# Mixture-of-experts layer on one core: down weights of an expert in one 4 MB transfer, the first chunk of the input projection by products, and new orders of units

## The reference

```python
h = rmsnorm(x, g_mix)
proj = h @ w_in                              # (256,1024) @ (1024,2048): u | q | k | v
y_pool = causal_multiscale_pool(u, w_pool, pool_scale)
y_attn = dilated_attention(q, k, v)          # 8 heads, three (window, dilation) patterns
x = x + concat(y_pool, y_attn) @ w_out
h2 = rmsnorm(x, g_ffn)
# top-4 of 32 experts for each token, softmax over the chosen logits -> combine[token, expert]
for e in range(32):
    gu = h2 @ w_gu[e] + b_gu[e]              # (256,1024) @ (1024,2048)
    gate = minimum(gu[:, :1024], 7); lin = clip(gu[:, 1024:], -7, 7)
    act = gate * sigmoid(1.702 * gate) * (lin + 1)
    out = out + combine[:, e:e+1] * (act @ w_down[e] + b_down[e])
return rmsnorm(x + out, g_final)
```

## Time and profile before

| | |
|---|---|
| time, median of 3 executions | 1023.37 us (1023.37 to 1024.65) |
| the profiled execution: its time | 1022.32 us |
| its span, first to last instruction | 1020.5 us |
| mean granted TensorE clock, share of full speed | 0.979 |
| TensorE busy | 957.0 us, 94% |
| VectorE, ScalarE busy | 285.6 us, 134.8 us |
| moved by DMA | 419.53 MB, 411 GB/s over the span |

### The profile page before, as it was taken

How to read it: one execution, slowest core, us unless ns; L and a number is a source line. 1 busy time by engine, 2 the same in 40 slices (tenths; PEclk the granted TensorE clock), 3 DMA queues, 4 the chain that set the end, 5 groups by cost and what they waited for, 6 DMA issues and landing times.

```text
span 1020.5 us, 11711 instructions
## 1 busy us (share of the span) xinstructions
PE 957.0 (94%) x4837; PEld 421.8 (41%) x4837; DVE 285.6 (28%) x536; ACT 134.8 (13%) x200; POOL 15.1 (1%) x17
## 2 busy tenths in 40 slices
PE   8999999999999998989899899989999898999996
PEld 8988443434343342424243243424324243434332
DVE  5963521313122113113122212212211311222123
ACT  6634200000101000000000000000100000010002
POOL 0500000000000000000000000000000000000000
PEclk9999999999999999999999899989999999999999
DMA  9578999999999999999999999999999999999995
GB/s 354 218 325 363 396 407 416 426 423 431 435 427 430 432 430 429 430 431 433 432 429 432 432 425 432 432 437 432 432 429 432 424 430 432 437 424 430 425 426 206
DMA packets 26321, 419.53 MB, mean 411 GB/s; under 512 B 4164, under 2 KB 4824, under 8 KB 8856
## 3 DMA queue, kind: packets, MB, share of 16 engines
q1 hardware_dynamic: 26256, 419.15, 96.8%
q10 hardware_dynamic: 40, 0.01, 0.0%
HBM read 418.11 MB, written 1.05 MB: 411 GB/s over the span
## 4 chain that ended last, share of the span: by engine, by line
PE 51%; DMA 44%; DVE 3%; ACT 1%; issue 0%; SPq 0%; DVEq 0%; ACTq 0%
PE ps L988 49%; DMA raw<-in_w_gu 40%; DMA raw<-in_w_down 3%; DVE woutl L720 1%; PE ps L1284 1%; PE ps L1234 1%; DMA win<-in_w_in 1%; ACT sm L538 0%; PE ps L1081 0%; DVE mxs L737 0%; DVE sm L732 0%; DVE xT L816 0%; PE ps L1135 0%; DVE acc L967 0%; DVE outs L970 0%
## 5 line engine op out<-in xcount | busy, mean ns | idle before, releaser
L988 PE MATMUL ps<-raw,xT 128*64 128x512 f32 x2032 | 469.8, 614 | 34.1 <-DMA raw<-in_w_gu 34.1
L988 PEld LDWEIGHTS ps<-raw,xT 128*64 128x64 f32 x2032 | 144.3, 141 | 339.2 <-issue 292.8
L988 PE MATMUL ps<-raw,actT 128*64 128x512 f32 x1024 | 232.1, 595 | 0.7 <-DMA raw<-in_w_down 0.7
L988 PEld LDWEIGHTS ps<-raw,actT 128*64 128x64 f32 x1024 | 70.6, 137 | 135.0 <-issue 132.4
L911 DVE TENSOR_TENSOR biased<-ps,biasT 128x1024 f32<-128x1024 f32 x32 | 39.2, 1224 | 304.1 <-PE ps L1234 304.1
L604 ACT ACTIVATE gu<-ps 128x1024 f32<-128x1024 f32 x32 | 32.8, 1025 | 551.2 <-PE ps L988 551.2
L928 DVE TENSOR_TENSOR acc<-ps,acc 128x512 f32<-128x512 f32 x60 | 38.8, 686 | 168.8 <-PE ps L988 168.8
L816 DVE TENSOR_TENSOR xT<-ps,gT 128x512 f32<-128x512 f32 x32 | 22.1, 692 | 166.0 <-PE ps L988 165.9
L988 PE MATMUL ps<-ysc,dispT 64*128 64x512 f32 x256 | 65.5, 613 | 0.9 <-ACT ysc L616 0.9
L988 PEld LDWEIGHTS ps<-disp,h 128*128 128x128 f32 x512 | 58.4, 192 | 12.4 <-issue 12.2
L988 PE MATMUL ps<-disp,h 128*128 128x128 f32 x512 | 61.7, 278 | 0.2 <-DVE disp L810 0.2
(11 more groups left out here) (161 smaller groups left out, 440.3 us busy)
## 6 DMA issues: line engine op xcount, KB each, us to landing
raw<-in_w_gu SPq DMA_DIRECT2D x57, 4096.0 KB, 33.2
raw<-in_w_down SPq DMA_DIRECT2D x63, 2048.0 KB, 31.4
raw<-in_w_gu SPq DMA_DIRECT2D x13, 2048.0 KB, 12.8
win<-in_w_in SPq DMA_DIRECT2D x16, 512.0 KB, 12.4
wout<-in_w_out SPq DMA_DIRECT2D x4, 1024.0 KB, 10.0
early<-in_w_gu SPq DMA_DIRECT2D x1, 2048.0 KB, 12.2
raw<-in_w_down SPq DMA_DIRECT2D x2, 1024.0 KB, 36.8
acc<-in_x SPq DMA_DIRECT2D x2, 512.0 KB, 4.0
```

Source lines behind the costliest of these rows:

```text
L988: return pe.matmul(out_, lhsT, rhs, start=start, stop=stop, skip_group_check=shared)
```

## The change

Seven things change.

1. **Down weights whole.** Where the two down units of an expert lie in neighbouring buffers (`whole_down`), `load_down_whole` fetches both in one 4 MB transfer with rows of 32 KB. It waits until the second of the two buffers is free, and TensorE's `down_unit` waits for the whole before the first unit. This holds for four of the six down loads of three pairs, the last expert's excepted, and for the one of pair 0, half 1: 20 of the 32 experts in all.
2. **First chunk by products.** `first_chunk` does all high-by-high products of chunk 0 first, then those with `hTl`, then those with `winl`, and waits for each part only when its products come. ScalarE and VectorE take the split of weight chunk 1 before the second part of the input.
3. **Chunks 0 and 1 of pair 0's second expert** are multiplied before the transposes of the routing weights and of the first gate-and-up result.
4. **The first piece for pair 1** comes in two halves of 1 MB (`load_halves`): the first is issued once chunk 0 is used (`half_unit`), the second once the unit is.
5. **Pair 1's second expert** comes in four 2 MB pieces (`small_next=second_loaded`) where two transfers of 4 MB stood.
6. **Down unit (0, 1) ahead of the wait for `xT_ready`** and of `turn_gu`, in all pairs but the last. In the last pair, down (1, 0) goes ahead of the wait for `outputs_ready` and the first `last_scatter`.
7. **The first three pairs of the loop are written out**, and the loop runs from 1: three rounds where four were.

```diff
+        def whole_down(third, half):
+            return buffer(0, third, 10 if half else 4) < RAW - 1
...
+            def load_halves(e, s):
+                src = w_gu[0, bass.ds(e, 1), 0:4 * P, :].rearrange("a (p r) n -> p (a r) n", r=4)
+                sp.wait_ge(half_unit, 1)
+                sp.dma_start(raw[:, s, 0, :], src[:, 0, :]).then_inc(halves_loaded[0], 16)
+                sp.wait_ge(unit_used, 1)
+                sp.dma_start(raw[:, s, 1, :], src[:, 1, :]).then_inc(halves_loaded[1], 16)
...
+            def load_down_whole(e, s, half):
+                sp.dma_start(raw[:, s:s + 2].rearrange("p b r n -> p (b r n)"),
+                             w_down[0, bass.ds(e, 1), :, :].rearrange("a (p r) n -> p (a r n)", r=8)).then_inc(
+                                 down_whole[half], 16)
...
+                elif j is None or whole_down(third, 1):
+                    free(i, k + 1)
+                    load_down_whole(a + 1, at_(k), 1)
                 else:
                     for u in range(DN_U):
                         down(a + 1, u, k + u, down_loaded[1])
                 if not last:
                     gate_up(nxt + 1, ITER_U, 1, small_next)
-                    down(nxt, 0, ITER_U + GU_U, down_loaded[0])
-            iteration(None, 0, small=third_loaded)
+                    if j is None or whole_down((third + 1) % 3, 0):
+                        free(i, ITER_U + GU_U + 1)
+                        load_down_whole(nxt, at_(ITER_U + GU_U), 0)
+                    else:
+                        down(nxt, 0, ITER_U + GU_U, down_loaded[0])
+            iteration(None, 0, small=third_loaded, small_next=second_loaded)
...
-            with sp.Fori(0, triples) as j:
+            for third in range(3):
+                iteration(0, third)
+            with sp.Fori(1, triples) as j:
...
             turned_high(0)
             win_part(0, 0)
+            win_part(0, 1)
             turned_high(1)
-            win_part(0, 1)
+            win_part(0, 2)
             turned_high(2)
+            win_part(0, 3)
             turned_high(3)
-            for c in range(2, 5):
-                win_part(0, c)
+            win_part(0, 4)
...
+            def first_chunk(parts):
+                for product, (w, x_) in enumerate(((winh, hTh), (winh, hTl), (winl, hTh))):
+                    if product == 1:
+                        pe.wait_ge(hTl_ready, 1)
+                    if product == 2:
+                        pe.wait_ge(win_low[0], 1)
+                    for bank, column in parts:
+                        for j in range(4):
+                            mm(ps[:, bank + j // 2, (j % 2) * T:(j % 2 + 1) * T],
+                               w[0][0][:, column + j * P:column + (j + 1) * P], x_[:, 0, :],
+                               start=product == 0 and j % 2 == 0, stop=False, shared=True)
...
+                ins = gu_unit(0, c, None if c >= 6 else 1 + c // 2, 1)
+                if c == 0:
+                    ins.then_inc(half_unit, 1)
+            for c in range(2):
+                gu_unit(1, c, buffer(None, 0, 0), 1, second_loaded)
...
-                    if k == 1:
+                    if k == (2 if first else 1):
                         pe.wait_ge(gate_clipped, i * 2 + 1)
                         pe.wait_ge(up_clipped, i * 2 + 1)
...
                     gather(1)
+                    down_unit(0, 1, buffer(j, third, 5), j, third)
                     pe.wait_ge(xT_ready, i * 2 + 4)
+                    turn_gu(i * 2 + 1)
                 else:
                     pe.wait_ge(dispT_ready, i + 1)
                     pe.wait_ge(added, i * 4 - 4 + (TT + 4))
-                turn_gu(i * 2 + 1)
-                down_unit(0, 1, buffer(j, third, 5), i + 1)
+                    turn_gu(i * 2 + 1)
+                    down_unit(0, 1, buffer(j, third, 5), j, third)
...
                 if last:
+                    down_unit(1, 0, buffer(j, third, 10 - gap), j, third, last=True)
                     pe.wait_ge(outputs_ready, i * 2 + 1)
                     last_scatter(0, 0)
-                    down_unit(1, 0, buffer(j, third, 10 - gap), i + 1, last=True)
-                    down_unit(1, 1, buffer(j, third, 11 - gap), i + 1, last=True)
+                    down_unit(1, 1, buffer(j, third, 11 - gap), j, third, last=True)
                     last_scatter(0, 1)
```

More of the change, by code:

```diff
@@ L392, in gate_up @@
                     if loaded is not None:
-                        for k in range(GU_U):
+                        if j is None and half == 0:
+                            load_halves(e, at_(first))
+                        for k in range(j is None and half == 0, GU_U):
                             free(i, first + k)
@@ L405, in iteration @@
                 k = GU_U
-                if j is not None:
+                if j is not None and not whole_down(third, 0):
                     down(a, 1, k + 1, down_loaded[0])
@@ L1005, in by_channel @@
             def by_channel(c, bank, h, column):
-                first, last = c == 0, c == DC - 1
+                last = c == DC - 1
                 for j in range(4):
@@ L1026, in _ @@
             pe.wait_ge(vec_ready, 1)
-            for c in range(DC):
+            pe.wait_ge(hTh_ready, 1)
+            pe.wait_ge(win_high[0], 1)
+            first_chunk(((6, DP), (4, 0)))
+            for c in range(1, DC):
                 pe.wait_ge(hTl_ready, c // 2 + 1)
@@ L1200, in gu_unit @@
                 r = c % 2
-                if pieces is not None:
+                if pieces is third_loaded and c < 2:
+                    pe.wait_ge(halves_loaded[r], 16)
+                elif pieces is not None:
                     if r == 0:
-                        pe.wait_ge(pieces[c // 2], 16)
+                        pe.wait_ge(pieces[c // 2], count * 16)
                 elif c % 4 == 0:
@@ L1260, in _, with iteration @@
             triples = pe.snap(pe.value_load(further[0:1, 0:1], min_val=0, max_val=MORE) + 4)
-            def iteration(j, third, last, first=False, biases=False):
+            def iteration(j, third, last, first=False, biases=False, pieces=None):
                 i = number(j, third)
                 for k in range(DC):
-                    gu_unit(1, k, buffer(j, third, k // 2), i, second_loaded if first else last_loaded if last else None)
-                    if k == 1:
+                    if not (first and k < 2):
+                        gu_unit(1, k, buffer(j, third, k // 2), pieces or i - 1, second_loaded if pieces else None)
+                    if k == (2 if first else 1):
                         pe.wait_ge(gate_clipped, i * 2 + 1)
@@ L1328, in last_scatter @@
                         ins.then_inc(scattered, 1)
-            iteration(None, 0, False, first=True)
-            with pe.Fori(0, triples) as j:
+            iteration(None, 0, False, first=True, pieces=1)
+            iteration(0, 0, False, pieces=2)
+            iteration(0, 1, False)
+            iteration(0, 2, False)
+            with pe.Fori(1, triples) as j:
                 for third in range(3):
```

42 lines of the change are left out of this document (28 added, 14 removed).

## The result

| | before | after |
|---|---|---|
| median | 1022.5 us (20 runs beside the change) | 1024.61 us (1022.37 to 1026.55, 20 runs) |
| ratio | | 1.002, 95% interval 1.0013 to 1.0026 |
| profiled execution: time | 1022.32 us | 1025.99 us |
| its span | 1020.5 us | 1024.2 us |
| mean granted clock | 0.979 | 0.982 |

The account below looks back on a forecast made before the run. The weight stream was taken to set the pace, TensorE close behind. From the profiled 1022.32 us, -1.3 - 1.1 - 1.6 + 0.7 + 2.0 gave 1021.0, plus 1.05 for the median: 1022.1 us, range 1018.0 to 1025.2.

Parts of the forecast that it names:

- Term 1: At the start, TensorE's first product begins at about 10.6 us instead of 11.94, shifting the whole stream: -1.3 us.
- Term 2: Weight stream from 105 to 177 us: 4.4 us of losses before, a new 3.3 us hole after: -1.1 us.
- Term 3: Down weights in 32 KB rows: 0.08 us saved on each of 20 whole transfers, -1.6 us.
- Rival C: Longer rows of `w_down` give nothing, so term 3 is 0: 1023.7 us, chance 0.11.
- Term 4: Three more pairs written out bring about seven more instruction fetches, delaying the slowest DMA engine: +0.7 us.
- Term 5: At the end, TensorE stands 2.85 us for pair 14's whole down transfer before down unit (1, 0): +2.0 us.
- rival B: Pair 14's stall brings the slow clock: +1.7 us, or +3.0 in the longer form (1025.1 us); chance 0.13.
- A: Pair 14's stall does not set the end; the tail costs 0.4 us: 1019.8 us, chance 0.26.
- D: Fixed cost holds in the queue too: 2 us saved for each of 20 transfers fewer, 983 us, chance 0.01.

Follow-up runs that it names:

- experiment 6: The kernel before with only down unit (0, 1) moved ahead of the wait for gathered tokens and the transposes; 1022.79 us, ratio 0.9995.
- experiment 4: The kernel before with only the first three pairs of the loop written out; 1024.29 us, ratio 1.0016.
- experiment 11: p2 with the first three pairs of the loop written out; 1019.62 us, ratio 0.9964 to the kernel before.
- experiment 5: The kernel before with only `first_chunk` and the new order of ScalarE's and VectorE's parts; 1022.09 us, ratio 0.9988.
- b1: The kernel before with only the same 20 whole down transfers added; 1023.8 us, ratio 1.0012.
- b4: Same run as experiment 4: the kernel before with only the first three pairs written out; 1024.29 us, ratio 1.0016.
- a1: The change with pair 14's down weights of half 1 in two transfers again; 1023.11 us, ratio 0.9999 to the kernel before.
- a3: The change with the first scatter again ahead of down unit (1, 0) in the last pair; 1024.27 us, ratio 1.0016 to the kernel before.
- p4: p2 with pair 0's whole down transfer of half 1 put back; 1021.17 us, ratio 0.9981 to the kernel before.
- a2: The change with all down weights in two transfers, no wholes; 1021.25 us, ratio 0.9991 to the kernel before.
- p1: The change without whole transfers, with the loop rolled and the last pair's old order; 1019.47 us, ratio 0.9962 to the kernel before.
- p2: p1 with 18 whole down transfers, all but pair 0's and pair 14's of half 1; 1017.48 us, ratio 0.9939 to the kernel before.
- p3: p2 with pair 14's whole down transfer of half 1 put back; 1022.02 us, ratio 0.9989 to the kernel before.
- p5: Same run as experiment 11: p2 with the first three pairs written out; 1019.62 us, ratio 0.9964 to the kernel before.
- (1): Same run as a1: the change with pair 14's half-1 down weights in two transfers again; 1023.11 us, ratio 0.9999 to the kernel before.
- (9): Same run as p3: p2 with pair 14's whole of half 1 put back; 1022.02 us, ratio 0.9989 to the kernel before.
- (10): Same run as p4: p2 with pair 0's whole of half 1 put back; 1021.17 us, ratio 0.9981 to the kernel before.

## Why the prediction was wrong

What bounds the kernel was read rightly. In experiment 6 the waits for tokens gave nothing, and in experiments 4 and 11 work that TensorE never waits for by name, the fetches, moved the end.

**Term 1, the start (-1.3): the way right, the size not shown.** An earlier first product does pass undiminished to the first full issue (97.3 us later in all six profiles without the slow stretch at 100 us, of both kernels). But the 11.94 that the sum started from is the latest of the four profiles without `first_chunk`, and the mean moved from 11.5 to 11.0 only. The medians of experiment 5 give 1.2, with 0.1 to 2.4. Not foreseen was that some executions drop to 1.2 GHz at 100 us, on both sides, which cost the change's profile 1.6 us.

**Term 2, the feeding (-1.1): half of it wrong.** The time from the first full issue to the landing of the mark sorts the 14 profiles:

| kernels | from the issue to the mark, us |
|---|---|
| before and its four edits (b1 to b4) | 86.67 to 86.98 |
| the change, a1, a3, p4: new order, pair 0's whole | 86.53 to 87.08 |
| a2, p1, p2, p3, p5: new order, no whole in pair 0 | 83.52 to 84.27 |

The means of the three rows are 86.9, 86.8 and 83.9. The new hole was forecast at 3.3 us and is 2.9, its issue at 131.4 (131.24 in p4), its landing at 144.9 (145.33). What was over-stated was the other side: the halves and small pieces win 3.0 us, not 4.4. The step that failed is the count of what "the stream lost", 0.7 and 3.7 us, all of which I took as saved. The landings of p1_plain tell which part was not (like that of the kernel before, its profile has no slow stretch in the routing). Its first piece for pair 1 lands 9.83 us after the issue (107.78 to 117.61), and so it does in the kernel before (109.22 to 119.05): the 0.7 did not come back. From there to the mark p1_plain takes 74.22 us and the kernel before 77.13, which is 2.9 of the 3.7. The reading of the earlier trace rows as transfers into an idle queue was wrong as well: they were issued at 125.45 and 152.58, while the transfers ahead landed at 128.82 and 154.98. They landed 5.35 and 11.09 us behind those, where their bytes take 4.9 and 9.75, so the two holes were of 0.5 and 1.3 us. The net is nothing, not -1.1. (The row b1 also has the whole in pair 0, and 86.98: with the old feeding, whose later 4 MB transfer left a hole of its own, it cost nothing more.)

**Term 3, the longer rows (-1.6): right.** -1.45 by the first engine's landings of the change, -1.39 in b1, and -1.23 between p1 and p2, which is 0.07 to 0.08 us for each transfer behind the mark. The medians of p1 and p2 are 2.0 us apart, with intervals that just overlap. Rival C is out.

**Term 4, the fetches (+0.7): the mechanism right, the size wrong.** Measured +1.64 in the profiles, 1.6 (0.6 to 2.7) in experiment 4, 2.1 in experiment 11 (1.2 by its gap). The step that failed is "a packet of 16 KB holds one of the 16 engines for 0.62 us". That is a packet of weights; one of instructions lasts 1.07 us, and six came in addition, not seven. And I took the middle of "falls on engines that are ahead" and "two on the slowest", while the trace has the gap grow by 1.6 us in the stretch of the six fetches and stay.

**Term 5, the end (+2.0): right in place and stall, short by the clock.** The stall was forecast at 2.85 and is 2.71. Left to rival B was what follows it: in all three profiles with this stall (the change, a3, p3: 2.71, 2.74, 2.72) the 16 matmuls behind it took 5.12 to 5.35 us. The sentence that failed is "the new stall in pair 14 is 2.85 us, between those", for which I let the likeliest case have no slow clock at all. In the change stall and slow matmuls make 4.2 us (2.71 + 1.52). Of these, 1.2 us went mostly into idle time that TensorE had before (0.50 and 0.21 us in the earlier trace rows, and a wait for `ysc` of 0.87 us there, which is now one of 0.48 us for `actT`), where the forecast had let 0.50 go, and +2.96 stood at the end. Where the stall was 1.64 us (b1), the clock held. No run has a stall of 2.7 us in the tail at the full clock, so how the 2.96 splits between the two is worked out and not measured. The Trainium skill (TensorE: Matmul & The Clock Gate, section on HAM oscillation) has matmuls that stand for a transfer go on at half rate. The three profiles agree at this place: 16 matmuls in 5.12 to 5.35 us instead of 3.60; in the middle of the program only some stalls do (last section).

**Together.** The last four rows of the table give -0.4, -1.5, +1.6 and +3.0, in sum +2.7, where the forecast had 0.0 (-1.1, -1.6, +0.7, +2.0). With a start between -0.5 (the means of the first product) and -1.2 (5) that is +1.5 to +2.2, against a measured +2.1 with 1.3 to 2.7. The forecast had the sign wrong because three terms were off by 0.7 (feeding), 0.9 (fetches) and 1.0 us (the end), all to the same side, and the start may have added up to 0.8. That 1024.61 lies inside the range is partly luck: its upper end was made for the longer form of rival B, and the time got there by the shorter form and two other errors.

**The rivals.** A (the gain reaches the end) is out: taking the stall away gives 2.1 us (1) and putting it back costs 4.5 by the medians and 3.7 by the traces (9). B came true as a mechanism, in its shorter form (1.5 us of slow matmuls, not 3.0). With the price of that form, 1.7, the forecast would have been 1023.8, with the longer one 1025.1; the 1024.61 measured lies between them, and 0.13 was too little for it. D is out: 18 transfers fewer gave 2.0 us between p1 and p2, not 36. The Trainium skill (DMA: Bandwidth & Descriptors, section on the anatomy of one DMA) gives 2.0 us of fixed cost for each DMA on the path through GpSimd, while SyncE issues these. By these runs no such cost shows for transfers that queue behind one another, since their landings stay 4.9 us apart for 2 MB.

**Open:** The medians put 3.7 us on pair 0's whole (10) where the stream shows 2.8. The differences against p2_mid_wholes in 9 (4.5 and 3.7), in 11 (2.1 and 1.2) and against p1_plain (2.0 and 1.2) stand off to the same side by 0.8 or 0.9 us, so its median, from 6 executions and with an interval of 1.6 us either way, is probably that much too low. Why the clock falls in the routing in some executions and not in others was not tried.

## What to carry to other kernels

A longer transfer saves little per byte (0.07 to 0.08 us for 4 MB here) and ties the first half of its data to the second, at both ends: it can't be issued until the second buffer is free, and can't be used until the second half has landed. Use it where the queue is deep and the consumer will wait later anyway, and split it where the queue runs dry and where nothing behind it has slack; with 2 of the 20 left alone, the loop rolled and the old order at the end, this kernel was 0.8% faster than the change and 0.6% faster than before. Unrolled code is traffic in a kernel that is bound by transfers, and a stall in the tail is to be priced with and without a slow clock behind it. A sum made against one profile takes over that profile's chance: the first product of the kernel before started anywhere from 11.12 to 11.94 us, and a change of 1 us at the start is within that.

## What the runs showed that I had not expected

- **A landing counts the slowest of 16 engines, and little of the gap between them is won back while the queue is full.** It was 1.96 us at 196 us and 3.40 at the end in the kernel before, 5.16 in the change. It grows in stretches where instructions are fetched, though not at each fetch, and stands nearly still in between (2.07 at 500, 2.04 at 790 in the kernel before, where no fetch falls). Only where the queue ran dry did it close: from 2.60 to 0.72 us between the landings at 112 and 146 us of the change. A fetch of 16 KB lasts 1.07 us on one engine, a row of weights of the same size 0.62.
- **A 4 MB transfer issued 1.3 us before the queue runs dry still leaves a hole of about 3 us** (p4: 12.8 us behind the piece ahead, for 9.75 us of bytes). A piece issued 5.3 us before it left none: at 126.95 in p1_plain, with 132.29 as the landing ahead, it landed at 137.22, 4.93 later. In the change itself the whole was issued at 133.55, 0.6 us after the piece ahead had landed (132.97): into an empty queue it took 12.3 us, 2.6 more than its bytes.
- **The clock falls at another place in each execution of nearly the same kernel.** Stalls of 2.05 and 2.62 us in the middle of the change had slow matmuls behind them, one of 2.42 and one of 2.72 not:

```profile
323.28 3.65 PE L1029 MATMUL ps<-raw,actT 128*64 128x512 f32 x16 [2.72 <-DMA raw<-in_w_down]
...
441.45 5.35 PE L1029 MATMUL ps<-raw,actT 128*64 128x512 f32 x16 [2.05 <-DMA raw<-in_w_down]
...
499.73 5.28 PE L1029 MATMUL ps<-raw,actT 128*64 128x512 f32 x16 [2.62 <-DMA raw<-in_w_down]
...
616.45 3.65 PE L1029 MATMUL ps<-raw,actT 128*64 128x512 f32 x16 [2.42 <-DMA raw<-in_w_down]
```

Of all 37 stalls of 2.60 to 2.75 us for weights in the 14 profiles, 18 had slow matmuls behind them and 19 had not. So the length of a stall alone doesn't decide there, and a forecast does well to give such a stall both prices, at about even chances.
